# Gate row moved from the weights to the finished row tiles in a seven-product output projection

## The reference

```python
# block 1; att: 512 columns of attention, mlstm_out: 512 columns, RMS-normed by head and gated
mix = concatenate([att, mlstm_out(h_sum, mo, mlstm_norm_w)], -1)
x = x + g1 * (mix @ w_out)              # g1: one row of 1024 gates, from the modulation vector
hx2 = modulate(rmsnorm(x, norm2_w), sh2, sc2)
aff = softmax(hx2 @ w_router, -1)       # the router reads the new x
```

## Time and profile before

| | us |
|---|---|
| time, median of 3 runs (lowest, highest) | 4063.98 (4062.65, 4070.71) |
| time of the profiled execution | 4068.23 |
| its span | 4066.5 |
| out1 (begin to begin of the next stage) | 1225 to 1504 |
| out2 | 3224 to 3494 |

### The profile page before, as it was taken

The page is one execution under the profiler, slowest core; times in us unless marked ns, Lnnn a source line. Parts: engine busy times, 40 slices in busy tenths (PEclk is TensorE's granted clock), DMA queues, the critical chain, the costliest instruction groups (busy, mean ns, idle before and its releaser), DMA issues. The chain is left out here.

```text
span 4066.5 us, 62341 instructions
## 1 busy us (share of the span) xinstructions
PE 3749.8 (92%) x21727; PEld 2429.4 (60%) x21728; DVE 2046.2 (50%) x4251; ACT 1535.3 (38%) x3413; POOL 703.0 (17%) x810
## 2 busy tenths in 40 slices
PE   6999999799897978999999799997999899599998
PEld 4667766555583434777776677774666545344444
DVE  1344333556596753111111268777333466578886
ACT  1122211355562431111111256764333223267775
POOL 0000000100174320111111001011000233322222
PEclk8999999899998988999999899998999999699999
DMA  6222122222524568656656212115221034488974
GB/s 240 78 80 79 70 80 75 87 72 85 145 96 169 178 244 314 206 166 208 205 165 217 68 52 62 59 53 148 68 81 62 22 127 141 178 314 281 329 241 102
DMA packets 227175, 574.09 MB, mean 141 GB/s; under 512 B 28155, under 2 KB 100987, under 8 KB 211119
## 3 DMA queue, kind: packets, MB, share of 16 engines
q1 hardware_dynamic: 177742, 395.92, 27.8%
q0 software_dynamic: 49248, 175.79, 14.6%
HBM read 433.59 MB, written 137.93 MB: 141 GB/s over the span
## 5 line engine op out<-in xcount | busy, mean ns | idle before, releaser
L884 PE MATMUL inp_psU<-inp_w,inp_hT 128*128 128x512 f32 (+3 forms) x1376 | 420.8, 464 | 0.0
L884 PEld LDWEIGHTS inp_psU<-inp_w,inp_hT 128*128 128x128 f32 x1376 | 256.0, 190 | 152.7 <-issue 122.4
L4499 DVE COPY moe_bu<-moe_wu 128x1024 f32 x480 | 299.1, 698 | 38.6 <-issue 19.6
L4386 PE MATMUL moe_psU<-moe_bu,shared_weights 128*32 128x256 f32 x3840 | 295.6, 383 | 1.1 <-issue 1.1
L4386 PE MATMUL moe_psU<-moe_wu,shared_weights 128*32 x1280 | 293.7, 383 | 1.1 <-DVE moe_bu L4499 1.1
L880 PE MATMUL inp_psU<-inp_hT,inp_w 128*128 128x256 f32 x1088 | 243.8, 384 | 9.3 <-DVE inp_tm L686 4.5
L3037 DVE TENSOR_TENSOR moe_hT<-moe_sg,moe_psG 128x256 f32<-128x256 f32 x64 | 27.0, 421 | 438.6 <-ACT moe_sg L3020 438.6
L3020 ACT ACTIVATE moe_sg<-moe_psG 128x256 f32<-128x256 f32 x64 | 24.6, 384 | 567.9 <-PE moe_psG L2979 567.9
L3715 PE MATMUL inp_psU<-shared_weights,inp_w 128*128 128x256 f32 x1024 | 232.3, 382 | 2.6 <-DMA inp_wg<-in_lru_wx 2.6
L880 PEld LDWEIGHTS inp_psU<-inp_hT,inp_w 128*128 128x128 f32 x1088 | 207.7, 193 | 41.2 <-issue 3.9
L2979 PE MATMUL moe_psG<-moe_xT,moe_u_w 128*128 128x256 f32 x1024 | 231.5, 379 | 0.0
(11 more groups left out here) (738 smaller groups left out, 7510.6 us busy)
## 6 DMA issues: line engine op xcount, KB each, us to landing
moe_wu<-in_w_up SPq DMA_DIRECT2D x32, 2048.0 KB
moe_d_w<-in_w_down SPq DMA_DIRECT2D x16, 2048.0 KB, 10.3
moe_wd<-in_w_down SPq DMA_DIRECT2D x32, 1024.0 KB
moe_u_w<-in_w_up SPq DMA_DIRECT2D x15, 2048.0 KB, 13.4
mod_w<-in_w_ada SPq DMA_DIRECT2D x24, 1024.0 KB, 11.4
inp_mod_w<-in_w_mod SPq DMA_DIRECT2D x16, 1024.0 KB, 5.1
xn<-out_xn POOLq DMA_DIRECT2D x32, 512.0 KB, 5.4
shared_weights<-in_w_gate SPq DMA_DIRECT2D x8, 2048.0 KB, 8.6
```

What stands on the lines that cost most here:

```text
L884: mm = pe.matmul(psU[:, u % NB, 0:n], hT[:, par, k, j * P:(j + 1) * P], w[:, k, lo:lo + n], start=(k == 0), stop=(k == KD - 1))
L4386: mm = pe.matmul(psU[c, f, 0:2 * P], xT[:, p, k, c], w, start=(k == 0), stop=(k == KD - 1), tile_position=(0, g * LOT))
L4499: ins = dve.tensor_copy(bu[:, g - 1, f, c, :].rearrange("p k n -> p (k n)").unsqueeze(1), wu[:, bass.ds(slots[g - 1], 1), f, c, :].rearran ...
```

## The change

The weights are no longer scaled. The gate row has a tile of its own, loaded within the stage (in out1 behind the rest of the weights), and is multiplied into each finished row tile on VectorE: in `first_rest` for the first two tiles, in the new `add_x` (a multiply of 128x1024, then the add of x) for the others. The four sums of weights are all made by VectorE (`make_right`), two before the pairs and two inside pair 1. The products of a pair are P1, P2, P6, P5, P3, P7, P4. `first_part(1)` comes ahead of `turn(0)`. ScalarE takes `root_mix` ahead of the second gate and, in a pair, `root_mix(d)` ahead of `keep_turned(b-2)` and `root_x(a)` ahead of `keep_across(b-2)` and `keep_mix(d)`. On GpSimd the scaling and two weight sums are gone. The diff, cut to its core:

```diff
-    P1, P2, P6, P7, P5, P3, P4 = range(7)
+    P1, P2, P6, P5, P3, P7, P4 = range(7)
...
+                sp.dma_start(gr[:, :], rows.gate_row.to_broadcast([P, D])).then_inc(gr_landed, 16)
...
+            def add_x(t):
+                j = t % 2
+                dve.wait_ge(summed, 4 * (t // 2) - 2 + 2 * j)
+                dve.tensor_tensor(xo[:, j, :], xo[:, j, :], gr[:, :], ALU.mult).then_inc(weighed, 1)
+                dve.wait_ge(weighed, t - 1)
+                dve.wait_ge(x_landed[j], nth(t))
+                dve.tensor_tensor(xo[:, j, :], xo[:, j, :], x[:, j, :], ALU.add).then_inc(x_added, 1)
+
             def finish(t):
                 j = t % 2
-                if t < 2:
-                    dve.wait_ge(taken, 2 * t + 2)
-                else:
-                    dve.wait_ge(summed, 4 * (t // 2) - 1 + j)
-                    dve.wait_ge(x_landed[j], nth(t))
-                    dve.tensor_tensor(xo[:, j, :], xo[:, j, :], x[:, j, :], ALU.add).then_inc(x_added, 1)
-                    dve.wait_ge(x_added, t - 1)
+                dve.wait_ge(x_added, t + 1)
...
             def first_rest(t):
                 dve.wait_ge(made, t + 1)
+                dve.wait_ge(gr_landed, 16)
+                for h in range(2):
+                    dve.tensor_tensor(xo[:, t, cols[h]], psO[:, t, h, :], gr[:, cols[h]], ALU.mult).then_inc(taken, 1)
+                dve.wait_ge(taken, 2 * t + 2)
                 dve.wait_ge(x_landed[t], 16)
-                for h in range(2):
-                    dve.tensor_tensor(xo[:, t, cols[h]], psO[:, t, h, :], x[:, t, cols[h]], ALU.add).then_inc(taken, 1)
-                finish(t)
+                dve.tensor_tensor(xo[:, t, :], xo[:, t, :], x[:, t, :], ALU.add).then_inc(x_added, 1)
+
+            def make_right(n):
+                if n == 1:
+                    dve.wait_ge(direct_weights_landed, 32)
+                    ins = dve.tensor_tensor(t1, w_direct[:, :, cols[1]], w_direct[:, :, cols[0]], ALU.subtract)
+                elif n == 2:
+                    dve.wait_ge(normed_weights_landed, 32)
+                    dve.wait_ge(right_made, 1)
+                    ins = dve.tensor_tensor(t2, w_normed[:, :, cols[1]], t1, ALU.subtract)
+                elif n == 3:
+                    dve.wait_ge(made, 2)
+                    ins = dve.tensor_tensor(w_direct[:, :, cols[1]], w_normed[:, :, cols[1]], w_direct[:, :, cols[1]], ALU.subtract)
+                else:
+                    dve.wait_ge(right_made, 2)
+                    ins = dve.tensor_tensor(t4, w_normed[:, :, cols[0]], t2, ALU.subtract)
+                ins.then_inc(right_made, 1)
 
             def join(q, i, to, other, done, n):
 
                 dve.wait_ge(made, made_by(q, i))
                 dve.wait_ge(parted, n)
-                return dve.tensor_tensor(to, bank(q, i), other, ALU.add).then_inc(done, 1)
-
-            dve.wait_ge(gr_landed, 16)
-            dve.wait_ge(direct_weights_landed, 32)
-            for h in range(2):
-                dve.tensor_tensor(w_direct[:, :, cols[h]], w_direct[:, :, cols[h]], gr[:, cols[h]].unsqueeze(1).to_broadcast([P, KH, BANK]),
-                                  ALU.mult).then_inc(direct_scaled, 1)
-            for t in range(2):
-                square_mix(t)
-                scale_mix(t)
-            dve.wait_ge(direct_scaled, 2)
-            dve.tensor_tensor(t1, w_direct[:, :, cols[1]], w_direct[:, :, cols[0]], ALU.subtract).then_inc(right_dve, 1)
+                dve.tensor_tensor(to, bank(q, i), other, ALU.add).then_inc(done, 1)
+
+            square_mix(0)
+            scale_mix(0)
+            square_mix(1)
+            scale_mix(1)
+            make_right(1)
             square_mix(2)
             scale_mix(2)
-            dve.wait_ge(normed_scaled, 2)
-            dve.wait_ge(right_dve, 1)
-            dve.tensor_tensor(t2, w_normed[:, :, cols[1]], t1, ALU.subtract).then_inc(right_dve, 1)
+            make_right(2)
             square_mix(3)
             scale_mix(3)
-            for t in range(2):
-                first_rest(t)
+            first_rest(0)
+            first_rest(1)
+            finish(0)
+            finish(1)
...
+                if q == 1:
+                    make_right(3)
                 if more:
                     scale_mix(c)
-                join(q, P7, part[:, 2, :], part[:, 1, :], parted, n + 2)
-                if more:
                     square_mix(d)
                 elif picks:
                     early_choice.choose_group(dve)
                 join(q, P5, part[:, 3, :], part[:, 1, :], parted, n + 2)
-                room(b)
-                join(q, P5, xo[:, 1, cols[1]], part[:, 2, :], summed, n + 3)
+                if q == 1:
+                    make_right(4)
                 if more:
                     scale_mix(d)
-                join(q, P3, xo[:, 0, cols[1]], part[:, 3, :], summed, n + 4)
+                join(q, P3, xo[:, 0, cols[1]], part[:, 3, :], summed, n + 3)
+                add_x(a)
                 finish(a)
+                room(b)
+                join(q, P7, xo[:, 1, cols[1]], part[:, 3, :], summed, n + 3)
+                join(q, P7, part[:, 2, :], part[:, 1, :], parted, n + 2)
                 join(q, P4, xo[:, 1, cols[0]], part[:, 2, :], summed, n + 4)
+                add_x(b)
                 finish(b)
...
             gate(0)
+            root_mix(0)
             gate(1)
-            root_mix(0)
             keep_mix(0)
             root_mix(1)
             keep_mix(1)
             gate(2)
+            root_mix(2)
             gate(3)
-            root_mix(2)
+            keep_mix(2)
             root_mix(3)
+            keep_mix(3)
             root_x(0)
-            keep_mix(2)
             root_x(1)
-            keep_mix(3)
             for q in range(1, PAIRS):
                 a, b, c, d = (2 * q + n for n in range(4))
                 more = q + 1 < PAIRS
                 elif picks:
                     early_choice.exponent(act, 0)
                 keep_across(a - 2)
+                if more:
+                    root_mix(d)
                 keep_turned(b - 2)
                 keep_logits(a - 2)
                 if more:
-                    root_mix(d)
                     keep_mix(c)
                 elif picks:
                     early_choice.exponent(act, 1)
+                root_x(a)
                 keep_across(b - 2)
                 if more:
                     keep_mix(d)
-                root_x(a)
                 keep_logits(b - 2)
                 root_x(b)
...
             first_part(0)
+            first_part(1)
             turn(0)
-            first_part(1)
             turn(1)
             first_product(0)
             first_product(1)
                 turn_xn(a - 2)
                 pe.wait_ge(mixT_ready, a + 1)
                 multiply(q, P2, normed_of(a), w_normed[:, :, cols[0]])
+                if q == 1:
+                    pe.wait_ge(right_made, 2)
                 pe.wait_ge(left_made, 4 * q - 2)
-                if q == 1:
-                    pe.wait_ge(right_dve, 2)
                 multiply(q, P6, left[:, 1, :, :], t2)
                 route_across(a - 2)
-                pe.wait_ge(left_made, 4 * q)
-                if q == 1:
-                    pe.wait_ge(right_pool, 2)
-                multiply(q, P7, direct_of(b), w_direct[:, :, cols[1]])
+                multiply(q, P5, left[:, 0, :, :], t1)
                 turn_xn(b - 2)
                 route(a - 2)
-                multiply(q, P5, left[:, 0, :, :], t1)
+                pe.wait_ge(left_made, 4 * q - 1)
+                multiply(q, P3, left[:, 2, :, :], w_normed[:, :, cols[1]])
                 if more:
                     turn(c)
-                multiply(q, P3, left[:, 2, :, :], w_normed[:, :, cols[1]])
+                if q == 1:
+                    pe.wait_ge(right_made, 3)
+                pe.wait_ge(left_made, 4 * q)
+                multiply(q, P7, direct_of(b), w_direct[:, :, cols[1]])
                 route_across(b - 2)
                 if more:
                     turn(d)
+                if q == 1:
+                    pe.wait_ge(right_made, 4)
                 multiply(q, P4, normed_of(b), t4)
...
-            pool.wait_ge(gr_landed, 16)
-            pool.wait_ge(normed_weights_landed, 32)
-            for h in range(2):
-                pool.tensor_tensor(w_normed[:, :, cols[h]], w_normed[:, :, cols[h]], gr[:, cols[h]].unsqueeze(1).to_broadcast([P, KH, BANK]),
-                                   ALU.mult).then_inc(normed_scaled, 1)
-            pool.wait_ge(normed_scaled, 2)
-            pool.wait_ge(right_dve, 2)
-            pool.tensor_tensor(t4, w_normed[:, :, cols[0]], t2, ALU.subtract).then_inc(right_pool, 1)
             make_left(1)
-            pool.wait_ge(made, 2)
-            pool.tensor_tensor(w_direct[:, :, cols[1]], w_normed[:, :, cols[1]], w_direct[:, :, cols[1]], ALU.subtract).then_inc(right_pool, 1)
             store(0)
```

(32 more changed lines are left out.)

14 lines of the change are left out of this document (5 added, 9 removed).

## The result

The changed kernel takes 4081.76 us (median of 6 runs, 4079.45 to 4084.91) where the kernel before takes 4067.32 (6 runs, 4062.65 to 4070.71): a ratio of 1.0038 with a 95% interval of 1.0025 to 1.0051, 14 us more. The profiled span grew from 4066.5 to 4081.8. The forecast of 4062 was wrong, and in the other direction: it is 19.8 us too low, of which 3.3 lie in its base (the kernel before at 4063.98 by three runs, 4067.32 by six) and the rest in the change.

What follows compares the result with a forecast made beforehand. TensorE was taken to bound the pairs (28.60 us each in out1). Terms -7.5 + 1 + 3.6 + 0 + 0 + 1.2 = -1.7, off the median 4063.98, gave 4062 us, range 4054 to 4071.

Steps and rivals of the forecast that it cites:

- The beginning of out1 up to P1, -7.7: Out1 ahead of the pairs: P1 of pair 1 at 1271.0 for 1278.69, 7.7 us earlier.
- To P4 of pair 1, -7.5 and +1: Out1 up to pair 1's P4: 7.5 us sooner (5 to 9.5), plus 1 (0 to 3) for two VectorE weight sums.
- The pairs of out1, +3.6: Out1's steady pairs: +0.6 us for each of six steps, +3.6 in all (0 to +9).
- slower: chain (1): Rival: the chain through the store decides out1's pairs, 31.1 us each, +15, 4074 in all; chance 0.10.
- Chain (1): Out1's pairs, from `room(a)` through VectorE, ScalarE, GpSimd's sums and the store's landing: 29.5 to 31.1 us, or 28.6.
- the ring: Out1's pairs: the chain through the store from one release of `room(a)` to the next, forecast at 28.6 to 31.1 us.
- The marker: Out1's pairs: TensorE waits ahead of `turn` and `route_across(b-2)` would show that the chain through the store decides.
- chain (2): Out1's pairs, through `keep_turned(a)` behind `root_x(b)` on ScalarE, with VectorE's steps: 28.3 to 29.3 us.
- VectorE beside GpSimd: Out1's pairs: GpSimd's sums can hold VectorE's multiplies; tile b's added multiply costs 1.8 us instead of 1.26.
- The end of out1, 0: After P4 of pair 7: one more multiply, 1.26, against `finish(a)` no longer behind `room(b)`; 0 (-2 to +1.5).
- Out2, 0 and +1.2: Out2: beginning 0 (-2.5 to +1.5), pairs kept at 29.51 us, and +1.2 for the bare multiply at the end.
- The beginnings win and the pairs don't pay: Rival: both chains in the pairs stay under 28.60 us; about -9, 4055; chance 0.16.

Runs made afterwards that it cites:

- experiments 3: Changed kernel, gate multiply left out of tile a, then in a second run of tile b: 4068.47 and 4060.32 us, one run each.
- experiment 4: Changed kernel with SyncE's two loads of direct rows issued ahead of the load of x for tile b: 4066.12 us, 0.9997 of before.
- experiment 2: Changed kernel with ScalarE's `root_x(a)` moved back behind `keep_mix(d)`: 4064.83 us, 0.9992 of before.
- experiment 1: Changed kernel with GpSimd's store of tile a issued ahead of `make_left` for the next pair: 4064.17 us, 0.9993 of before.
- the second pair: The changed kernel and the kernel before traced once more, both unedited: 4079.90 us for the changed one, spans differing by 9.2 us.

## Why the prediction was wrong

*The beginning of out1 up to P1, -7.7:* right, -6.9. *To P4 of pair 1, -7.5 and +1:* came out at -4.2 together, for -6.5. The first `turn_xn` came 54.7 us after the begin, at the late end of the 53.2 to 55 foreseen: half of what is missing. Beyond it TensorE waited 0.64, 1.24 and 1.14 us inside pair 1, for VectorE's normed tiles and ScalarE's logits. VectorE works there without a gap from 1287.19 to 1302, with the two weight sums of 2.28 us in it, so the term of 1 was too small as well. (The 21.5 us of work after `turn_xn(0)` hold five products, not the six I wrote; the sum is right with five.)

*The pairs of out1, +3.6:* this is the step that failed. I took +0.6 for each of six; it measured +14.9 in all, the size I had given the rival "slower: chain (1)" (+15, six pairs of 31.1), at 1 in 10. That the rival's 31.1 is so near is luck: it was made of sums of 8.3, 1.3 too long, and a landing of 6.3, 0.8 to 2.3 too short. Chain (1) was the right chain and its parts on the engines were right or long: VectorE 15.1 (measured 14.94), ScalarE 1.4 (1.18), GpSimd 7.4 to 8.3 (7.03). The landing was wrong: "4.7 to 6.3", read from a kernel in which the loads go out 2.8 us ahead of the store, was 7.1 to 8.6. These are the loads ahead of the store at 1347.66, before:

```profile
1344.41 0.33 SPq L1034 DMA_DIRECT2D shared_rows<-in_x  x1
1344.84 0.93 SPq L1030 DMA_DIRECT2D out_mixT<-attT  x2
```

I named the case ("the store now shifts towards the loads") and did not price the shift. Its size could have been worked out: the sums take 7.03 us for 8.32 (I had allowed for 7.4), which brings the store 1.3 us sooner, and the loads, behind the multiply and the add of b, go out 6.4 us after the begin of the sums for 5.5, 0.9 later. Together that is the 2.2 us from 2.8 to 0.6. What the landing becomes at that distance no row of the kernel before shows. With 4.7 for the landing the ring is 27.9, with 5.3 it is 28.5, and TensorE's 28.60 decides, as in experiments 3 and 4; with 6.3 it is 29.5.

The marker was wrong too: I named waits ahead of `turn` and `route_across(b-2)` for chain (1). The wait came ahead of `route(a-2)`, since `root_mix(c)` stands before `keep_across(a-2)` on ScalarE. TensorE also waits 0.33 to 0.36 us for `out_h2T` in four of the six pairs, where I expected such a wait in each. That does not show chain (2) to be as long as sized (28.3 to 29.3): in experiments 2 and 4, with pairs of 28.6, TensorE never waits for `out_h2T` in these pairs, so chain (2) was not over 28.6 there.

*VectorE beside GpSimd:* the multiply of b took 1.60 us (I had said 1.8), the add 2.20, the square 2.17, for 1.22 to 1.23 each in tile a. That a VectorE instruction with two SBUF inputs and a GpSimd one that reads SBUF hold each other up is what the Trainium skill states (SBUF — State Buffer, "Who interferes with whom"), and the trace agrees: GpSimd's sums run from 1369.40 to 1376.43. I had placed the cost in chain (2); it acted on the loads, which wait for the add.

*The end of out1, 0:* -0.7 from P4 of pair 7 to the next stage's first matmul. A late store held P7 of pair 7 for 1.06 us, for the 1 I allowed. *Out2, 0 and +1.2:* -0.1 in the first pair of traces (beginning -1.25, pairs 29.51 as said, end +1.1) and +1.9 in the second, 287.1 to 289.0. The size was right; the single -0.1 says little.

*The rivals.* "The beginnings win and the pairs don't pay" (4055) is what experiments 1, 2 and 4 make, at 4064 to 4066, 1 to 3 us under the kernel before: out1 gains 6 us, and out2 nothing (288.5 to 289.6).

*Left open:* the medians differ by 14.4 us (10 to 21 by the interval), the ends of out1 by 7.4 and 9.6 in two pairs of traces, out2 by -0.1 and 1.9. The 11.5 us of the second pair lie within the interval; a further 3 us outside the changed stages are neither shown nor ruled out, since one unchanged stage alone varies by nearly 6 with the granted clock. Nor is it shown why the landing depends on the loads as it does. Both sides give way: over the pairs of out1 (1330 to 1480 us) the direct loads land in a median of 4.3 us before, 6.0 in the changed kernel and 4.1 in experiment 4, the store of `xn` in 5.4, 7.7 and 4.7.

## What to carry to other kernels

Of a ring through a store take the landing from a place where it has the neighbours it will have: ask which loads are released by the instruction that you lengthen, and how far from the store they will then be issued. Issue a store as soon as its data stand, ahead of other work on the issuing engine; where a queue's order closes a ring, moving one small instruction back can be worth more than all that was saved elsewhere. And when TensorE waits at the beginning of a stage, look at what is queued behind a copy on the engine in between: here that, together with VectorE's order, brought 23 us over experiment 1 on unscaled weights; with the weights still scaled ScalarE's order alone brought 1 to 2 us in out1.

## What I had not expected of the hardware

One and the same 1 MB store (two DMAs of 512 KB) landed in 4.4 to 8.6 us, by the distance to some 1 MB of loads from another queue; experiment 4, which moves half of these loads alone, took it from 7.8 to 5.3. I had taken such a landing as 4.7 to 6.3. Over a shift of 2.2 us against the loads (2.8 to 0.6) it went from 4.6 to 4.9 in most pairs to 7.1 to 8.6. The last release of `room(a)` in out1 says the same. Beside its store go ten loads of 1 MB each of the next stage's weights. It landed in 13.3 us in the changed kernel, where the first of them was issued 0.7 us ahead of it, and in 7.1 in experiment 2, where it was issued 1.5 us behind it.
